# Twelve early down products spread over twelve pairs: one 128-expert tile of each, where both tiles of six pairs were made early, in a layer of pooling, window attention and product-key experts on one Trainium2 core

## The chip, the cores and the metric

The kernel runs on one core of one Trainium2 chip. The metric is the device time of one execution in microseconds (us), and the time of a kernel is the median of its runs. TensorE is the matrix engine, VectorE, ScalarE and GpSimd the other three that compute; SyncE (SP) issues most of the DMAs. In rows of the profile they are PE (PEld for its weight loads), DVE, ACT, POOL and SP.

## What is computed

One layer for 1024 tokens of width 1024, all in float32. First a mixer (a projection, multi-scale pooling, window attention with sinks, sigmoid gates, an output projection), then the product-key experts, then a norm:

```python
x = x + merged @ w_out[l]
x = x + peer_layer(rms_norm(x, g_ffn[l]), ...)
return rms_norm(x, g_final)

# peer_layer: 8 heads pick 16 of 128*128 experts for each token
gates = jax.nn.softmax(vals, axis=-1)
u = jnp.take(expert_down, eb, axis=0)
act = jax.nn.gelu(jnp.einsum('td,thkd->thk', hb, u).astype(jnp.float32))
wv = (gb * act).astype(expert_up.dtype)
vv = jnp.take(expert_up, eb, axis=0)
return jnp.einsum('thk,thkd->td', wv, vv)
```

So each token needs, for its 128 chosen experts, a dot product with a row of `expert_down` and a weighted sum of rows of `expert_up`.

## The kernel before

The eight blocks of 128 tokens are served in two ways. Three blocks (`DB = 3`) go **by rows**: for each of 128 choices GpSimd gathers one row of 4 KB per token (512 KB in all) by an indirect DMA, and VectorE forms the dot product (kind "dot", L1672) or adds the weighted row (kind "up", L1684). That is 3 x 2 x 128 = 768 rows (`NROW`), in the order block 0 dot, block 0 up, block 1 dot and so on. Five blocks (`ND = 5`, 640 tokens, `DT`) go **densely**: all 16384 experts are multiplied, and a table of gates, zero for experts not chosen, weights the result.

The dense work runs over `NPAIR = 64` pairs of tiles; pair p has the tiles (p, 0) and (p, 1), each of 128 experts. For a tile, the down product makes `abank` (experts x 640 tokens) in two halves of 256 and 384 tokens (`SPLIT`), 8 x 3 matmuls each. Three matmuls stand in for one of full precision: each float32 operand is split into a high part (ScalarE's copy to float32r: `tdown_hi`, L1569; `tup_hi`, L1577; `w_hi`, L1595) and a low part (the difference: `tdown_lo`, L1482, and `tup_lo`, L1486, on GpSimd; `w_lo`, L1724, on VectorE). ScalarE takes the gelu of `abank` into `w` (L1588), VectorE multiplies by the gates (`weights`, L1720) and makes the low part (`weights_rest`, L1724). The up product of the pair (`up_product`, L1546 to L1548) goes over five token blocks t, 12 matmuls of 512 columns each, into `ybank`, of which two pairs exist; VectorE adds each to `y` (`add_y`, L1731).

The order on each engine is written out. TensorE, for pair p: the first half of tile (p+1, 0), up product t = 0, second half, t = 1, first half of (p+1, 1), t = 2, second half, t = 3, t = 4. VectorE: the last addition of pair p-1, then five parts of the pair's rows in shares 3, 2, 1, 3, 1, with an addition, the weights of (p+1, 0), an addition and their low part, an addition, the weights of (p+1, 1), an addition and their low part between them. GpSimd: four parts of the gathers in shares 2, 3, 2, 3, followed by `down_rest(p+1, 1)`, `up_rest(p+1, 0)`, `down_rest(p+2, 0)` and `up_rest(p+1, 1)`; the gathers go into a ring of eight rows (`RU = 8`). ScalarE makes the high parts and gelus in the matching order. `rows_of_pair` deals the 768 rows to the pairs by `SHARE`.

**Early down products.** While the mixer's last work runs, TensorE has room. There the mixer makes the down products of twelve tiles (`PRE`, `NPRE`), keeps them in DRAM (`scr["pre"]`), and in the experts' loop those tiles are left out of the loads, the splits and `down_half`; instead SP loads the result into `w` (`load_pre`, L1413), and ScalarE's gelu works on it in place (L1582). The pair ahead of an early pair (where its down product would have been made) gets fewer rows. It is called a light pair here.

Who waits for whom is counted by semaphores that only rise: `down_low` and `down_high` (splits done), `a_ready` (a down product done), `gl_ready` (a gelu done), `w_ready`, `w_low`, `y_ready`, `y_added`. Since early tiles don't count in some of them, `normal(p)` gives how many pairs ahead of p are not early.

Of the kernel before, what the change touches and what calls it, by code (L numbers as in the profile page):

```python
# [11 lines left out]
NG = T // TG  # L12
# [61 lines left out]

PRE = list(range(4, NPAIR, 10))
NPRE = 2 * len(PRE)
LAST = NG * NTILE + NPRE

# [39 lines left out]
def mixer(nc, io, scr):  # L118

    with ExitStack() as ctx:  # L120
# [233 lines left out]
        def _(sp):  # L354
# [4 lines left out]
            def load_tile(n):  # L359
                if n >= RING:  # L360
                    sp.wait_ge(w_low, n - RING + 1)
                g, i = divmod(n, NTILE)
                src = io["tiles"][i] if g < NG else io["downT"][2 * PRE[i // 2] + i % 2]
                sp.dma_start(raw[:, n % RING], src).then_inc(tile_in[n % RING], 16)
# [917 lines left out]

SHARE = [3 if p + 1 in PRE else 10 for p in range(NPAIR)]

# [71 lines left out]

def normal(p):

    return p - sum(n < p for n in PRE)


def experts(nc, io, scr, kept, late):
# [8 lines left out]
    with ExitStack() as ctx:  # L1371
# [32 lines left out]
        def _(sp):  # L1404
            def load_tdown(p, q):
                if p in PRE:
                    return
                sp.wait_ge(down_low, 2 * (normal(p) - 1) + q + 1)
                sp.dma_start(tdown[:, q], io["downT"][2 * p + q]).then_inc(tdown_in[q], 16)

            def load_pre(p, q):
                sp.wait_ge(w_low, 2 * (p - 1) + q + 1)
                sp.dma_start(w[:, q], scr["pre"][2 * PRE.index(p) + q]).then_inc(pre_in[q], 16)  # L1413

# [25 lines left out]
            for p in range(NPAIR):  # L1440
# [7 lines left out]
                if p + 3 < NPAIR:  # L1448
                    load_gates(p + 3)
                if p + 2 in PRE:  # L1450
                    for q in range(2):
                        load_pre(p + 2, q)
# [17 lines left out]
        def _(pool):  # L1470
# [7 lines left out]
            def down_rest(p, q):  # L1478
                if p in PRE:
                    return  # L1480
                pool.wait_ge(down_high, 2 * normal(p) + q + 1)
                nc.gpsimd.tensor_tensor(tdown_lo[:, q], tdown[:, q], tdown_hi[:, q].bitcast(F32), ALU.subtract).then_inc(down_low, 1)  # L1482
# [33 lines left out]
        def _(pe):  # L1516
            def down_half(p, q, half):
                if p in PRE:
                    return
                if half == 0:  # L1520
                    pe.wait_ge(down_low, 2 * normal(p) + q + 1)
                    if q:
                        pe.wait_ge(gl_ready, 2 * p + 1)
                    elif p:
                        pe.wait_ge(gl_ready, 2 * (p - 2 if p - 1 in PRE else p - 1) + 2)
                a, b = SPLIT[half]
# [34 lines left out]
        def _(act):  # L1561
            def down_high_of(p, q):

                if p in PRE:
                    return
                act.wait_ge(tdown_in[q], 16 * (normal(p) + 1))
                if p:
                    act.wait_ge(a_ready, 2 * (normal(p) - 1) + q + 1)
                nc.scalar.activation(tdown_hi[:, q], tdown[:, q], ACT.Copy).then_inc(down_high, 1)  # L1569
# [9 lines left out]
            def expert_gelu(p, q):  # L1579
                if p in PRE:  # L1580
                    act.wait_ge(pre_in[q], 16 * (PRE.index(p) + 1))
                    nc.scalar.activation(w[:, q], w[:, q], ACT.Gelu_apprx_tanh).then_inc(gl_ready, 1)  # L1582
                    return
                act.wait_ge(a_ready, 2 * normal(p) + q + 1)
                if p:
                    act.wait_ge(w_low, 2 * (p - 1) + q + 1)
                for half, (a, b) in enumerate(SPLIT):
                    ins = nc.scalar.activation(w[:, q, a * P:b * P], abank[:, half, 0:(b - a) * P], ACT.Gelu_apprx_tanh)  # L1588
                ins.then_inc(gl_ready, 1)
# [270 lines left out]
```

## Time and profile before

| | us |
|---|---|
| median of 3 runs | 3027.0 |
| lowest, highest | 3024.17, 3028.58 |
| profiled execution | 3019.19 |
| its span (first to last instruction) | 3017.4 |

The profiled execution is one more run. Around its span lie 1.8 us. The mean granted clock of TensorE is 0.972 of full speed. Of the span TensorE is busy 94%, VectorE 77%, ScalarE 31%, GpSimd 70%; the experts' loop runs from about 1243 us to 3003 us. How to read the rows: times are us from the start of the span; an instruction's row has its start, its length, engine, line and operation, what it writes and reads, and in brackets the idle time of its engine before it with what ended it. A mean over the whole span says little here, as the mixer and the loop have different limits; a row of a stretch or of an instruction has to be read with its place in the pair.

### The profile page before, as it was taken

Reading aid. Unit: us, or ns where it says so; the run is one execution under the profiler, and the core shown is the slowest. Engines: PE = TensorE matmul, PEld = TensorE weight load, DVE = VectorE, ACT = ScalarE, POOL = GpSimd, SP = SyncE. Lnnn points to the kernel's source line nnn. Section 1 sums busy time; section 2 is a strip of 40 time slices with the busy share of each in tenths; the row PEclk is TensorE's granted clock in tenths of the full one; section 3 lists DMA queues with packets and bytes.
Section 4 is the critical chain, followed back from the end, with each engine's and each line's share of the span. In section 5 each row is a group of like instructions: output and inputs, shape, how many; then the busy total and the mean of one; then the engine's idle time right before and its main releaser. Section 6 shows DMA issues by size and latency. Waiting matters only on the chain.

```text
span 3017.4 us, 40171 instructions
## 1 busy us (share of the span) xinstructions
PE 2844.6 (94%) x15235; PEld 2477.6 (82%) x15235; DVE 2336.3 (77%) x4348; ACT 937.1 (31%) x1356; POOL 2124.3 (70%) x1552
## 2 busy tenths in 40 slices
PE   7999898999899799899999998999999989999996
PEld 6678777677689688889998997899899979989995
DVE  1332298345499899588999999898899979889998
ACT  4232433232332399322222222222222222222221
POOL 4324576338568799778887886888688868878883
PEclk9899999899899899999999999999999999999998
DMA  3112412112322377989998997999899979989996
GB/s 140 43 63 91 168 64 70 42 50 98 112 87 94 120 238 237 332 310 330 347 349 315 342 336 289 335 342 341 311 343 336 346 266 339 348 311 341 335 337 219
DMA packets 267584, 717.92 MB, mean 238 GB/s; under 512 B 20864, under 2 KB 104064, under 8 KB 267392
## 3 DMA queue, kind: packets, MB, share of 16 engines
q0 software_dynamic: 110912, 403.75, 35.8%
q1 hardware_dynamic: 156480, 311.61, 30.6%
q8 instruction: 121, 1.98, 0.2%
q14 instruction: 71, 0.58, 0.1%
HBM read 657.86 MB, written 57.41 MB: 237 GB/s over the span
## 4 chain that ended last, share of the span: by engine, by line
PE 34%; DVE 8%; POOL 7%; DMA 6%; issue 3%; ACT 1%; DVEq 0%; SPq 0%; ACTq 0%
PE abank L1530 6%; PE abank L1532 6%; PE abank L1531 6%; PE ybank L1546 6%; PE ybank L1547 5%; PE ybank L1548 5%; POOL up L1475 3%; DVE acc L1684 3%; DMA up<-in_down,e_idx 3%; POOL tdown_lo L1482 2%; DMA up<-in_up,e_idx 2%; DVE up L1672 2%; DVE e_y L1731 1%; POOL tup_lo L1486 1%; DMA w<-all_pre 1%
## 5 line engine op out<-in xcount | busy, mean ns | idle before, releaser
L1530 PE MATMUL abank<-m_hT,tdown_hi 128*128 128x384 f32 (+1 forms) x1856 | 576.4, 311 | 15.0 <-ACT w L1588 9.0
L817 POOL TENSOR_TENSOR m_wlo<-m_raw,m_whi 128x1024 fp32r<-128x1024 f32 x128 | 309.5, 2425 | 379.9 <-ACT m_whi L622 376.7
L1532 PE MATMUL abank<-m_hT,tdown_lo 128*128 128x384 f32 (+1 forms) x1856 | 575.9, 310 | 0.0
L1531 PE MATMUL abank<-m_hlo,tdown_hi 128*128 128x384 f32 (+1 forms) x1856 | 574.9, 310 | 0.0
L1546 PE MATMUL ybank<-tup_hi,w_hi 128*128 128x512 f32 x1280 | 509.1, 398 | 45.5 <-DVE e_y L1731 32.7
L1684 DVE SCALAR_TENSOR_TENSOR acc<-up,e_act,acc 128x1024 f32<-128x1024 f32 x381 | 489.7, 1285 | 65.9 <-DMA up<-in_up,e_idx 43.4
L1672 DVE CUSTOM_DVE_ANT_0 up<-up,acc 128x1024 f32<-128x1024 f32 x384 | 457.0, 1215 | 97.8 <-DMA up<-in_down,e_idx 95.2
L1547 PE MATMUL ybank<-tup_lo,w_hi 128*128 128x512 f32 x1280 | 506.2, 396 | 0.0
L1548 PE MATMUL ybank<-tup_hi,w_lo 128*128 128x512 f32 x1280 | 504.2, 394 | 0.0
L1475 POOL DMA_INDIRECT up<-in_up,e_idx x384 | 396.9, 1033 | 106.0 <-issue 92.4
L1475 POOL DMA_INDIRECT up<-in_down,e_idx x384 | 399.1, 1039 | 99.3 <-issue 88.9
L1731 DVE TENSOR_TENSOR e_y<-e_y,ybank 128x512 f32<-128x512 f32 x640 | 408.9, 678 | 5.3 <-PE ybank L1548 4.5
L1530 PEld LDWEIGHTS abank<-m_hT,tdown_hi 128*128 128x128 f32 x1856 | 353.9, 191 | 25.1 <-issue 10.0
L1531 PEld LDWEIGHTS abank<-m_hlo,tdown_hi 128*128 128x128 f32 x1856 | 354.6, 191 | 9.9
L1482 POOL TENSOR_TENSOR tdown_lo<-e_tdown,tdown_hi 128x1024 fp32r<-128x1024 f32 x116 | 281.4, 2426 | 112.6 <-ACT tdown_hi L1569 110.6
L1486 POOL TENSOR_TENSOR tup_lo<-e_tup,tup_hi 128x1024 fp32r<-128x1024 f32 x128 | 308.3, 2409 | 66.7 <-ACT tup_hi L1577 64.7
L1588 ACT ACTIVATE w<-abank 128x256 f32<-128x256 f32 x232 | 88.9, 435 | 856.5 <-PE abank L1532 693.5
L1532 PEld LDWEIGHTS abank<-m_hT,tdown_lo 128*128 128x128 f32 x1856 | 353.6, 191 | 0.0
L436 PE MATMUL bank<-m_hT,m_whi 128*128 128x512 f32 (+2 forms) x848 | 326.7, 385 | 11.6 <-POOL m_wlo L817 7.9
L1546 PEld LDWEIGHTS ybank<-tup_hi,w_hi 128*128 128x128 f32 x1280 | 244.1, 191 | 98.6 <-DVE e_y L1731 38.0
L438 PE MATMUL bank<-m_hT,m_wlo 128*128 128x512 f32 (+2 forms) x848 | 319.7, 377 | 0.0
L437 PE MATMUL bank<-m_hlo,m_whi 128*128 128x512 f32 (+2 forms) x848 | 319.3, 377 | 0.0
(226 smaller groups left out, 4714.6 us busy)
## 6 DMA issues: line engine op xcount, KB each, us to landing
e_tup<-in_up SPq DMA_DIRECT2D x128, 512.0 KB
m_raw<-in_tiles SPq DMA_DIRECT2D x116, 512.0 KB, 3.3
e_tdown<-in_downT SPq DMA_DIRECT2D x116, 512.0 KB
gates<-all_table SPq DMA_DIRECT2D x64, 640.0 KB
all_table<-t_out SPq DMA_DIRECT2D x9, 4096.0 KB, 14.7
m_raw<-in_downT SPq DMA_DIRECT2D x12, 512.0 KB, 3.7
up<-in_down,e_idx POOLq DMA_INDIRECT x384
up<-in_up,e_idx POOLq DMA_INDIRECT x384
```

Of the source, the lines that this page charges most:

```text
L1475: nc.gpsimd.indirect_dma_start(up[:, n % RU], None, io["up" if kind == "up" else "down"], bass.IndirectOffsetOnAxis(idx[:, b, k:k + 1], 0) ...
L1482: nc.gpsimd.tensor_tensor(tdown_lo[:, q], tdown[:, q], tdown_hi[:, q].bitcast(F32), ALU.subtract).then_inc(down_low, 1)
L1486: nc.gpsimd.tensor_tensor(tup_lo[p % 2][:, q], tup[:, q], tup_hi[p % 2][:, q].bitcast(F32), ALU.subtract).then_inc(up_low, 1)
L1530: nc.tensor.matmul(out, tdown_hi[:, q, at], h2T_hi[:, k, a:b], start=k == 0, stop=False)
L1531: nc.tensor.matmul(out, tdown_hi[:, q, at], h2T_lo[:, a:b, at], start=False, stop=False)
L1532: ins = nc.tensor.matmul(out, tdown_lo[:, q, at], h2T_hi[:, k, a:b], start=False, stop=k == KD - 1)
L1546: nc.tensor.matmul(out, w_hi[r][:, q, ts], tup_hi[r][:, q, ds], start=q == 0, stop=False)
L1547: nc.tensor.matmul(out, w_hi[r][:, q, ts], tup_lo[r][:, q, ds], start=False, stop=False)
L1548: ins = nc.tensor.matmul(out, w_lo[r][:, q, ts], tup_hi[r][:, q, ds], start=False, stop=q == 1)
L1672: nc.vector.tensor_tensor_reduce(out=src, in0=src, in1=h2_row[:], scale=1.0, scalar=0.0, op0=ALU.mult, op1=ALU.add, accum_out=act_of[:, b, ...
L1684: nc.vector.scalar_tensor_tensor(out=acc[:], in0=src, scalar=act_of[:, b, k:k + 1], in1=acc[:], op0=ALU.mult, op1=ALU.add).then_inc(row_us ...
L1731: nc.vector.tensor_tensor(part, part, ybank[n % 2 * 2 + i][:], ALU.add).then_inc(y_added, 1)
```

## The change

`PRE` is now a list of tiles: tile 0 of the pairs 4, 9, 14, ... 59. Twelve tiles are made early, as before, but they were both tiles of the pairs 4, 14, ... 54. The pair ahead of each takes 6 shares of rows where it took 3, a full pair 10. That is 592 shares in all where there were 598: 12.97 rows in a full pair (12.84), 7.78 in a light one (3.85). `normal` gives way to four functions that count tiles: how many computed tiles stand ahead of (p, q) in the order of the loop (`nth`), how many of the same q (`nth_in`), the count at which the last computed tile of the same buffer was done (`last_in`), and the last computed tile before this one (`last_before`). All waits on `down_low`, `down_high`, `a_ready`, `tdown_in`, `pre_in` and `gl_ready` are put through them. The orders on the engines are the same.

```diff
-PRE = list(range(4, NPAIR, 10))
-NPRE = 2 * len(PRE)
+PRE = [(p, 0) for p in range(4, NPAIR, 5)]
+NPRE = len(PRE)
...
-                src = io["tiles"][i] if g < NG else io["downT"][2 * PRE[i // 2] + i % 2]
+                src = io["tiles"][i] if g < NG else io["downT"][2 * PRE[i][0] + PRE[i][1]]
...
-SHARE = [3 if p + 1 in PRE else 10 for p in range(NPAIR)]
+SHARE = [6 if (p + 1, 0) in PRE else 10 for p in range(NPAIR)]
...
-def normal(p):
-
-    return p - sum(n < p for n in PRE)
+def nth(p, q):
+
+    return 2 * p + q - sum(tile < (p, q) for tile in PRE)
+
+
+def nth_in(p, q):
+
+    return p - sum(tile[1] == q and tile < (p, q) for tile in PRE)
+
+
+def last_in(p, q):
+
+    return nth(*max((n, q) for n in range(p) if (n, q) not in PRE)) + 1
+
+
+def last_before(p, q):
+
+    return max((n, r) for n in range(p + 1) for r in range(2) if (n, r) < (p, q) and (n, r) not in PRE)
...
             def load_tdown(p, q):
-                if p in PRE:
+                if (p, q) in PRE:
                     return
-                sp.wait_ge(down_low, 2 * (normal(p) - 1) + q + 1)
+                sp.wait_ge(down_low, last_in(p, q))
...
-                sp.dma_start(w[:, q], scr["pre"][2 * PRE.index(p) + q]).then_inc(pre_in[q], 16)
+                sp.dma_start(w[:, q], scr["pre"][PRE.index((p, q))]).then_inc(pre_in[q], 16)
...
-                if p + 2 in PRE:
-                    for q in range(2):
+                for q in range(2):
+                    if (p + 2, q) in PRE:
                         load_pre(p + 2, q)
...
             def down_half(p, q, half):
-                if p in PRE:
+                if (p, q) in PRE:
                     return
                 if half == 0:
-                    pe.wait_ge(down_low, 2 * normal(p) + q + 1)
-                    if q:
-                        pe.wait_ge(gl_ready, 2 * p + 1)
-                    elif p:
-                        pe.wait_ge(gl_ready, 2 * (p - 2 if p - 1 in PRE else p - 1) + 2)
+                    pe.wait_ge(down_low, nth(p, q) + 1)
+                    if 2 * p + q:
+                        n, r = last_before(p, q)
+                        pe.wait_ge(gl_ready, 2 * n + r + 1)
```

The same pattern is applied to `down_rest`, `down_high_of` and `expert_gelu`.

## Rows read from the trace of the kernel before

**Rows 1.** The page, busy tenths in 40 slices of the span, TensorE.

```profile
PE   7999898999899799899999998999999989999996
```

**Rows 2.** Waits of TensorE from 1240 us on: total us, times, longest.

```profile
PE ybank L1546 <- DVE e_y L1731: 32.7, 10, 6.5
PE ybank L1546 <- DVE w_lo L1724: 12.7, 8, 2.8
PE abank L1530 <- ACT w L1588: 7.1, 1, 7.1
```

**Rows 3.** Windows: stretch, us, busy PE, PEld, DVE, ACT, POOL; PEclk, DMA share, GB/s.

```profile
1299.50:1347.70 48.20, 43.69 (x219) 37.74 (x218) 39.93 (x63) 11.54 (x16) 32.38 (x24) 0.96 0.84 304
1571.10:1617.60 46.50, 43.18 (x219) 37.57 (x218) 42.09 (x47) 11.77 (x16) 30.91 (x23) 0.96 0.85 309
1850.30:1897.30 47.00, 42.32 (x218) 36.41 (x217) 41.10 (x62) 11.55 (x16) 31.00 (x24) 1.00 0.89 334
2120.60:2169.80 49.20, 44.08 (x217) 37.73 (x218) 40.05 (x47) 11.54 (x16) 32.81 (x25) 0.97 0.82 295
2392.60:2452.60 60.00, 46.63 (x218) 39.62 (x217) 47.14 (x67) 15.67 (x20) 35.33 (x26) 0.89 0.76 284
2675.50:2723.20 47.70, 43.64 (x218) 37.53 (x217) 42.04 (x63) 11.78 (x16) 32.06 (x25) 0.96 0.85 313
1812.50:1850.30 37.80, 30.70 (x158) 27.86 (x157) 33.48 (x47) 10.59 (x14) 23.84 (x18) 0.86 0.69 240
1645.40:1673.30 27.90, 27.90 (x159) 25.44 (x158) 25.54 (x27) 6.80 (x10) 23.39 (x18) 1.00 0.94 337
```

**Rows 4.** Timeline of TensorE in pair 16, a full one: start us, us.

```profile
1645.42 0.39 PE L1546 MATMUL ybank<-tup_hi,w_hi 128*128 128x512 f32 x1
...
1648.17 0.34 PE L1530 MATMUL abank<-m_hT,tdown_hi 128*128 128x384 f32 x1
...
1652.36 0.39 PE L1546 MATMUL ybank<-tup_hi,w_hi 128*128 128x512 f32 x1
...
1670.39 0.28 PE L1530 MATMUL abank<-m_hT,tdown_hi 128*128 128x256 f32 x1
...
1673.27 0.39 PE L1546 MATMUL ybank<-tup_hi,w_hi 128*128 128x512 f32 x1
```

**Rows 5.** Timelines of GpSimd, VectorE and TensorE in light pair 13 (starts 1596.0).

```profile
1600.34 2.40 POOL L1482 TENSOR_TENSOR tdown_lo<-e_tdown,tdown_hi 128x1024 fp32r<-128x1024 f32 x1 [0.49 <-ACT tdown_hi L1569]
1602.89 1.36 POOL L1475 DMA_INDIRECT up<-in_up,e_idx  x1
...
1608.50 1.29 DVE L1684 SCALAR_TENSOR_TENSOR acc<-up,e_act,acc 128x1024 f32<-128x1024 f32 x1 [3.09 <-DMA up<-in_up,e_idx]
...
1610.44 0.80 PE L1546 MATMUL ybank<-tup_hi,w_hi 128*128 128x512 f32 x1 [3.32 <-DVE e_y L1731]
```

**Rows 6.** Timeline of TensorE where light pair 3 starts.

```profile
1326.73 0.80 PE L1546 MATMUL ybank<-tup_hi,w_hi 128*128 128x512 f32 x1 [2.06 <-DVE w_lo L1724]
1327.32 0.63 PE L1547 MATMUL ybank<-tup_lo,w_hi 128*128 128x512 f32 x1
```

**Rows 7.** Timelines of GpSimd and VectorE late in full pair 16.

```profile
1667.43 2.42 POOL L1482 TENSOR_TENSOR tdown_lo<-e_tdown,tdown_hi 128x1024 fp32r<-128x1024 f32 x1
1670.04 0.82 DVE L1720 TENSOR_TENSOR w<-w,gates 128x640 f32<-128x640 f32 x1
```

**Rows 8.** Timeline of VectorE in pair 54, where rows turn from dot to up.

```profile
2723.96 2.37 DVE L1679 TENSOR_TENSOR e_act<-e_act,e_gate 128x128 f32<-128x128 f32 x1 [0.45 <-ACT e_act L1613]
```

**Rows 9.** Timelines of VectorE and GpSimd late in pair 12, ahead of light pair 13.

```profile
1593.09 0.82 DVE L1720 TENSOR_TENSOR w<-w,gates 128x640 f32<-128x640 f32 x1
1593.82 1.28 DVE L1731 TENSOR_TENSOR e_y<-e_y,ybank 128x512 f32<-128x512 f32 x2
1595.02 0.82 DVE L1724 TENSOR_TENSOR w_lo<-w,w_hi 128x640 fp32r<-128x640 f32 x1
...
1597.44 2.41 POOL L1486 TENSOR_TENSOR tup_lo<-e_tup,tup_hi 128x1024 fp32r<-128x1024 f32 x1 [10.88 <-ACT tup_hi L1577]
```

More of the change, by code:

```diff
@@ L1478, in down_rest @@
             def down_rest(p, q):
-                if p in PRE:
+                if (p, q) in PRE:
                     return
-                pool.wait_ge(down_high, 2 * normal(p) + q + 1)
+                pool.wait_ge(down_high, nth(p, q) + 1)
                 nc.gpsimd.tensor_tensor(tdown_lo[:, q], tdown[:, q], tdown_hi[:, q].bitcast(F32), ALU.subtract).then_inc(down_low, 1)
@@ L1517, in down_half @@
             def down_half(p, q, half):
-                if p in PRE:
+                if (p, q) in PRE:
                     return
                 if half == 0:
-                    pe.wait_ge(down_low, 2 * normal(p) + q + 1)
-                    if q:
-                        pe.wait_ge(gl_ready, 2 * p + 1)
-                    elif p:
-                        pe.wait_ge(gl_ready, 2 * (p - 2 if p - 1 in PRE else p - 1) + 2)
+                    pe.wait_ge(down_low, nth(p, q) + 1)
+                    if 2 * p + q:
+                        n, r = last_before(p, q)
+                        pe.wait_ge(gl_ready, 2 * n + r + 1)
                 a, b = SPLIT[half]
@@ L1562, in down_high_of @@
             def down_high_of(p, q):
-                if p in PRE:
+                if (p, q) in PRE:
                     return
-                act.wait_ge(tdown_in[q], 16 * (normal(p) + 1))
+                act.wait_ge(tdown_in[q], 16 * (nth_in(p, q) + 1))
                 if p:
-                    act.wait_ge(a_ready, 2 * (normal(p) - 1) + q + 1)
+                    act.wait_ge(a_ready, last_in(p, q))
                 nc.scalar.activation(tdown_hi[:, q], tdown[:, q], ACT.Copy).then_inc(down_high, 1)
@@ L1579, in expert_gelu @@
             def expert_gelu(p, q):
-                if p in PRE:
-                    act.wait_ge(pre_in[q], 16 * (PRE.index(p) + 1))
+                if (p, q) in PRE:
+                    act.wait_ge(pre_in[q], 16 * (p - nth_in(p, q) + 1))
                     nc.scalar.activation(w[:, q], w[:, q], ACT.Gelu_apprx_tanh).then_inc(gl_ready, 1)
                     return
-                act.wait_ge(a_ready, 2 * normal(p) + q + 1)
+                act.wait_ge(a_ready, nth(p, q) + 1)
                 if p:
```

## The prediction, made before the changed kernel was run

> **What bounds the kernel now.** I read the slices of the page first. From the sixteenth of forty the work is the experts' loop over 64 pairs, and there TensorE is busy nine tenths and more [rows 1]. The waits of TensorE in that loop come next [rows 2]: 52.5 us in all, and they have three kinds. 32.7 us (ten times) end with a VectorE addition into y (L1731), 12.7 us (eight times) with the low part of the weights (w_lo, L1724), and 7.1 us once with a gelu of ScalarE (L1588). Then the windows from pair to pair [rows 3]. A "pair" below is the stretch from the first up product of pair p (L1546) to that of pair p+1. A full pair takes 27.9 us with TensorE busy for all of it. The six stretches that hold a light pair (3, 13, ... 53, the pairs ahead of an early one) and the pair before it take 48.2, 46.5, 47.0, 49.2, 60.0 and 47.7 us, together 298.6, at clocks of 0.89 to 1.00. The reader should see that nothing is lost in full pairs and that almost all of the loss sits in these six and in pair 21.
>
> **What TensorE needs.** In a full pair [rows 4] the first up product starts at 1645.42, the larger half of the first down product at 1648.17, the second up product at 1652.36; the smaller half of the next down product at 1670.39, and the next pair at 1673.27. So the larger half costs 4.19 us, the smaller 2.88, one down tile 7.07, and the whole pair 27.85. The smaller half of tile 0 lies at the end of the pair before. Two down tiles gone make a two-pair stretch of 2 x 27.85 - 14.14 = 41.56 us; one gone makes 48.63, split as 24.97 (before) and 23.66 (light). Floor of today's six: 6 x 41.56 = 249.4. Their loss is 298.6 - 249.4 = 49.2 us; pair 21 loses 37.8 - 27.85 = 9.95. Sum of losses today: 59.2. The floor of the whole loop doesn't change: twelve tiles are left out either way, so **the change can only move the 59.2**.
>
> **Part 1, the mixer.** Twelve early tiles are loaded, split, multiplied and stored as before; only their addresses differ. Nothing, both ends nothing: same counts and sizes.
>
> **Part 2, inside the light pair.** Today a light pair needs 27.85 - 4.19 - 7.07 = 16.6 us of TensorE, but its y additions come late. The trace of pair 13 shows why [rows 5]: GpSimd has two low parts back to back with almost no gathers, so the gather at 1602.89 lands for VectorE only at 1608.50 (5.6 us later, 3.09 idle), the addition behind it is late, TensorE waits 3.32 us at 1610.44, and its clock then falls. After the change the light pair lasts 23.66 us and has 8 rows in VectorE's parts of 2, 2, 0, 3, 1. With s its start: the y additions of the previous pair to s+1.3, two rows and two additions to 5.1 (1.3 us a row, 1.28 two additions, 0.82 the weights and w_lo each [rows 5, 9]), two rows to 7.7, weights 8.5, additions 9.8, w_lo 10.6, first of three rows 11.9. The next two come from gathers behind one more gather and the tdown_lo that starts 4.3 us into pair 13 [rows 5], 5.0 to 7.4 after the change: at about s+7.5 and 9.1, and land 5.6 us later: 13.1 and 14.7, so the rows end at 16.0 and the additions at 17.3. TensorE needs them for its last up product at 4 x 2.75 + 7.07, about s+18. It is in time by 0.7 us; with landings 1.5 us later (the DMAs carry 8 rows where there were 4) it waits 0.8. I take 0.4 us for each of twelve, bounds 0 and 2: 5 us (0 to 24), where today the ten waits of this kind average 3.3.
>
> **Part 3, the entry.** Before a light pair TensorE lacks the 2.88 us of the small half and is ready for the next up product after 24.97 us, while VectorE and GpSimd still have a full pair's work. Today this is the w_lo wait: eight, 12.7 us, 1.6 each, up to 2.8 [rows 2, 6]; there will be twelve such entries where there are six. A second thing is new. Tile 1 of the early pair is now computed, so GpSimd makes its low part in the entry, behind the gelu that follows the larger half. In a full pair [rows 7] that tdown_lo runs 1667.43 to 1669.85, 22.0 to 24.4 us into the pair, and VectorE's weights start right behind it, at 1670.04. Where the two meet, VectorE's instruction ends only after GpSimd's: a multiply of just 128 x 128 takes 2.37 us [rows 8]. At today's entry of pair 12 GpSimd is idle for 10.88 us [rows 9]; the weights start at 1593.09 (22.0 us into the pair), and with two additions and w_lo VectorE is through at 1595.84, 2.75 us later, just before TensorE gets there at 24.97. With tdown_lo in that place (0.5 earlier than in a full pair, since GpSimd stands waiting: 21.5 to 23.9) VectorE goes on at 23.9 and is through at 26.7: TensorE is 1.7 us late. An entry where VectorE arrives later than 23.9 loses nothing to this, and is late by the old amount, 2.2 at pair 2 (27.2 us to the product at 1326.73 [rows 6] from the start at 1299.5 [rows 3]). I take 1.8 for each of eleven (the twelfth is pair 42's, part 5): 20 us. Bounds 0.8 and 2.8: 9 to 31.
>
> By the Trainium skill, page "SBUF — State Buffer", section "SBUF: two separate sides", VectorE and GpSimd share a port pair under an exclusive lock, and a VectorE op with two SBUF inputs that meets a GpSimd op waits for the whole instruction. By that rule every entry is held as above; without it an entry would cost what it costs today, about 1.2, and the entries together 13 us instead of 20. The 2.37 us multiply [rows 8] agrees with the rule.
>
> **Part 4, clock.** The granted clock falls to 0.5 (1.2 of 2.4 GHz) after some waits: after the entry wait of 2.06 us a product lasts 0.63 us [rows 6] where it lasts 0.39 in a full pair [rows 4], and of the six stretches only the one at 1850.3 averages 1.00 [rows 3]. The light pairs' waits over 3 us do it too [rows 5]. In a stretch of 48.2 us at 0.96, 1.9 us are lost to it; I take 1.8 a drop. With waits of 1.8 I expect one at two or three entries: 4 us (bounds 0 and 21, a drop at each).
>
> **Part 5, ends of blocks.** With 768 rows over 592 shares instead of 598, rows 256 and 512 still end in pairs 21 and 42, at the same places. Pair 21 keeps its 9.95 us (7.1 of it the gelu wait [rows 2]). Pair 42 keeps its y wait of 6.5 us, the longest of that kind [rows 2], and the low clock behind it, 3 us (of the 6.6 us that 0.89 takes from 60.0 [rows 3] about half): together 9.5, its entry included. What pair 43 loses beside it (today's 60.0 against 48 elsewhere) has its cause in the starved gathers of part 2 and mostly goes. Row 640, where VectorE turns from dot products to sums, moves from pair 54 into light pair 53; ScalarE's gelu and the multiply [rows 8] put some 3 us into VectorE's line there: 2 us more for TensorE. The same turn leaves pairs 31 and 32 about 2 us behind, as today (49.2 against 47 [rows 3]).
>
> **Part 6, queues.** SP's load of the precomputed tile now waits for w_lo of tile 0 only, which is long done; the wait for tile 1's, which held the loads queued behind it (tdown and tup of later pairs), goes. The new wait counts follow the same orders of tiles. Full pairs get 13 rows a little more often than 12: VectorE is busy 25.5 of 27.9 us and DMA 0.94 at 337 GB/s [rows 3], so VectorE's idle time covers it (0.13 row of 1.3 us, 0.17 us a full pair, if that is gone). A light pair moves 5 gathers and one tile fewer in 7.1 us less, 6.8 MB or 325 GB/s over 20.8 us, not above a full pair.
>
> **Sum.** 5 (light) + 20 (entries) + 4 (clock) + 9.95 + 9.5 (block ends) + 2 (row 640) + 2 (pairs 31, 32) = 52.5 us of loss where there is 59.2: 7 us gained. Against the profiled execution's own 3019.2 us this is 3012; the median of the runs shown is 3027.0, 7.8 above it, so **3020 us**.
>
> **Rivals.** (a) *All waits fold into the slack*: VectorE reaches the weights ahead of GpSimd, or after it without harm; entries 0.8 us each, light pairs 0, no drops. 9 + 23.5 = 33 of loss, 26 gained: 3001. For it: pair 12 today enters with no wait [rows 9]. Against: the w_lo waits average 1.6 [rows 2]. (b) *The entries take back the gain*: TensorE waits twelve times where it waited six, each near 2.4 us, and the clock falls after each (1.8 more): 11 x 4.2 = 46, and 5 + 23.5: 75, 16 lost: 3043. It decides from 2.8 us an entry, clock included: 11 x 2.8 + 5 + 23.5 is today's 59.2. For it: a wait of 2.06 brought the clock down [rows 6]. Against: w_lo waits average 1.6 [rows 2]. (c) *The gathers stay late in the light pair*: 0.6 us more in each, 12 x 0.6: the gain is gone and the time stays at 3027. (d) *It doesn't do what it says*: had the early tiles not been dropped from TensorE's line the loop would grow by 7.07 us each, to 3112; the conditions on (p, q) in all four engines agree, so I give it nothing.
>
> **How the numbers follow.** The forecast's case gets 0.45, (a) 0.16, (b) 0.20, (c) 0.19. The forecast's own range, 3012 to 3027, comes from entries between 1.1 and 2.4 us. To hold 8 in 10 it reaches to (a) and (b): 3001 to 3043. About 0.2% (6 us) is what a measurement can tell from no change. Faster: (a) and two thirds of the forecast's case (0.30), together 0.46, and 0.01 of (c): 0.47. Same: the rest of the forecast's case (0.15) and 0.15 of (c): 0.30. Slower: (b) and the bad end of (c): 0.23.
>
> **What would show it.** Right: no y wait over 1.5 us in light pairs outside 43 and 53; twelve entries, each with a w_lo wait of 1 to 2 us; GpSimd's tdown_lo just ahead of VectorE's weights in them; two-pair stretches near 51 us; pairs 21 and 42 as before. Wrong: entry waits under 0.5 or over 2.5, a clock below 0.97 in most stretches, waits for gathers over 1 us in the light pairs' three rows, or any wait of TensorE in full pairs.

## The result, and the profile after

| | before | after |
|---|---|---|
| median of the runs | 3025.4 us (6 runs, 3022.7 to 3028.6) | **3041.4 us** (6 runs, 3032.1 to 3045.8) |
| profiled execution: time, span | 3019.2, 3017.4 us | 3043.1, 3041.3 us |
| TensorE waits from 1240 us on: y, w_lo, gelu | 32.7, 12.7, 7.1 us [rows 2] | 33.4, 28.6, 6.9 us |

The ratio is 1.0047 (95% interval 1.0032 to 1.0061): slower by about 14 us (the medians lie 16 apart). The forecast was 3020 and faster. The time lies inside its range, close to the upper end, on the wrong side of no change.

The page of after (engine totals, then TensorE's slices) shows the same work with more time around it:

```profile
PE 2851.4 (94%) x15235; PEld 2477.7 (81%) x15235; DVE 2336.6 (77%) x4348; ACT 937.1 (31%) x1356; POOL 2124.6 (70%) x1552
...
PE   7999899999899799999999998999999989999996
```

The waits of TensorE from 1240 us on (total us, times, longest) answer to [rows 2]:

```profile
PE ybank L1560 <- DVE e_y L1745: 33.4, 18, 7.3
PE ybank L1560 <- DVE w_lo L1738: 28.6, 14, 2.9
PE abank L1544 <- ACT w L1602: 6.9, 1, 6.9
```

The w_lo waits rose from eight to fourteen, 12.7 to 28.6 us. That was forecast in kind. The y waits were to fade and did not: 18 of them, 33.4 us.

Windows of after from pair to pair (columns as in [rows 3]): entry 2 and light 3, entry 12, light 13 and full 14, entry 57 and light 58.

```profile
1296.90:1323.70 26.80, 25.21 (x135) 22.41 (x133) 23.35 (x40) 5.86 (x9) 19.08 (x15) 1.00 0.84 329
1323.70:1348.70 25.00, 24.09 (x133) 21.24 (x134) 21.86 (x33) 6.82 (x9) 20.81 (x16) 1.00 0.95 345
1568.20:1596.10 27.90, 25.16 (x135) 22.36 (x133) 25.24 (x27) 5.85 (x9) 19.95 (x16) 1.00 0.85 329
1596.10:1623.50 27.40, 25.63 (x132) 22.34 (x133) 21.28 (x25) 6.67 (x9) 19.27 (x14) 0.94 0.80 282
1623.50:1651.40 27.90, 27.90 (x159) 25.45 (x158) 24.34 (x26) 6.80 (x10) 23.07 (x18) 1.00 0.96 345
2827.20:2855.40 28.20, 25.29 (x134) 22.31 (x132) 25.24 (x27) 5.86 (x9) 20.05 (x17) 1.00 0.85 332
2855.40:2886.70 31.30, 28.50 (x133) 24.55 (x134) 23.31 (x26) 6.78 (x9) 21.35 (x15) 0.84 0.83 290
```

The forecast's floors serve as a ruler: 24.97 us for an entry, 23.66 for a light pair, 27.85 for a full one. (Where both tiles are early, a light pair's floor is 41.56 - 24.97 = 16.59.) A full pair stands on its floor, 27.9. Entries run 26.8 to 28.2, these lights 25.0 to 31.3. Summed over the loop's first 63 pairs, length less floor, in us:

| kernel (profiled execution) | entries | lights | full | sum |
|---|---|---|---|---|
| before | 18.4 | 30.9 | 11.2 | 60.5 |
| after | 38.5 | 36.5 | 12.0 | 87.0 |
| forecast for after | 20 + 9.5 (pair 42) | 5 + 2 (row 640) | 9.95 + 2 | 48.5, and 4 of clock |

Before is the 59.2 of the forecast, counted over all pairs. The 26.5 us more than before are the whole difference of the two profiled executions (23.9; the loop of after starts 2.6 us earlier). The medians differ by 16 only, since before's profiled execution is 6 us under its median and after's 2 over: some 8 of the 26.5 us are chance. Of the 34.5 us by which the forecast (52.5) missed, 25 to 29 lie in the light pairs and 9 in the entries.

### The profile page after: what moved, and what is told of

Its sections match the earlier page's. It is cut to its first block, busy times and chain, and to the rows that moved or that the text cites. A ratio compares the mean times of both kernels' runs of the same rounds, so it can differ in the third digit from the quotient of the medians.

```text
span 3041.3 us, 40171 instructions
## 1 busy us (share of the span) xinstructions
PE 2851.4 (94%) x15235; PEld 2477.7 (81%) x15235; DVE 2336.6 (77%) x4348; ACT 937.1 (31%) x1356; POOL 2124.6 (70%) x1552
## 4 chain that ended last, share of the span: by engine, by line
PE 15%; DVE 10%; DMA 10%; POOL 8%; issue 5%; ACT 2%; SPq 0%; DVEq 0%; ACTq 0%
POOL up L1490 4%; DMA up<-in_up,e_idx 4%; DMA up<-in_down,e_idx 4%; DVE acc L1698 4%; DVE up L1686 3%; PE abank L1544 3%; PE abank L1546 3%; PE abank L1545 3%; POOL tdown_lo L1497 3%; PE ybank L1560 3%; DMA w<-all_pre 2%; PE ybank L1561 2%; PE ybank L1562 2%; DVE e_y L1745 2%; POOL tup_lo L1501 1%
## 5 line engine op out<-in xcount | busy, mean ns | idle before, releaser
L1560 PE MATMUL ybank<-tup_hi,w_hi 128*128 128x512 f32 x1280 | 512.5, 400 | 62.1 <-DVE e_y L1745 33.4
L436 PE MATMUL bank<-m_hT,m_whi 128*128 128x512 f32 (+2 forms) x848 | 326.7, 385 | 11.9 <-POOL m_wlo L817 8.1
```

The lines of the kernel that those rows point to most:

```text
L1560: nc.tensor.matmul(out, w_hi[r][:, q, ts], tup_hi[r][:, q, ds], start=q == 0, stop=False)
```

## The experiments

All but e10 and e12 start from the kernel after. Ratios are to the kernel before.

**e1: the precomputed tile's load ahead of the gates.** In the light pairs of after one chain is late. Timelines of pairs 12 and 13 of after (13 starts at 1596.1; start us, us, engine and line; in brackets idle time and what ended it): SP's issues, ScalarE, GpSimd, VectorE, TensorE.

```profile
1594.07 0.33 SPq L1437 DMA_DIRECT2D gates<-all_table  x1
1594.44 0.43 SPq L1428 DMA_DIRECT2D w<-all_pre  x1
...
1603.80 0.74 ACT L1596 ACTIVATE w<-w 128x640 f32<-128x640 f32 x1 [8.04 <-DMA w<-all_pre]
1604.44 1.04 ACT L1583 ACTIVATE tdown_hi<-e_tdown 128x1024 fp32r<-128x1024 f32 x1
...
1605.56 2.68 POOL L1497 TENSOR_TENSOR tdown_lo<-e_tdown,tdown_hi 128x1024 fp32r<-128x1024 f32 x1 [5.92 <-ACT tdown_hi L1583]
1608.38 1.36 POOL L1490 DMA_INDIRECT up<-in_up,e_idx  x1
...
1614.45 2.68 DVE L1698 SCALAR_TENSOR_TENSOR acc<-up,e_act,acc 128x1024 f32<-128x1024 f32 x2 [4.33 <-DMA up<-in_up,e_idx]
...
1617.77 0.50 PE L1560 MATMUL ybank<-tup_hi,w_hi 128*128 128x512 f32 x1 [1.77 <-DVE e_y L1745]
```

SP issues the load of the precomputed tile right behind the gates' load, and it lands 9.4 us after its issue, for the gelu at 1603.80 (7.7 us into the pair). ScalarE takes its work in the order written, so the high part of tdown stands behind that gelu, for which ScalarE idles 8.04 us; GpSimd does too, so the low part (5.92 idle) and the gathers behind it wait as well; VectorE idles 4.33 for a row, and the y addition behind the row holds TensorE 1.77. In pair 13 of before the load was issued at 1594.31 and its gelu ran 4.3 us later (timelines of SP and ScalarE of before):

```profile
1594.31 1.88 SPq L1413 DMA_DIRECT2D w<-all_pre  x2
...
1598.58 0.74 ACT L1582 ACTIVATE w<-w 128x640 f32<-128x640 f32 x1 [1.22 <-DMA w<-all_pre]
```

There tdown_lo starts at 1600.34 and the gather is issued at 1602.89 [rows 5], against 1605.56 and 1608.38 here. Over all: in before the first of the two loads reaches its gelu in 4.3 to 4.8 us; in after it takes 4.8 to 6.3 us in the five light pairs ahead of which GpSimd issues two gathers in the entry's last 6 us, and 7.7 to 9.8 in the seven with three. e1 moves the load alone:

```diff
+                for q in range(2):
+                    if (p + 2, q) in PRE:
+                        load_pre(p + 2, q)
                 if p + 3 < NPAIR:
                     load_gates(p + 3)
-                for q in range(2):
-                    if (p + 2, q) in PRE:
-                        load_pre(p + 2, q)
```

> Edit: on the SP queue the load of the precomputed tile is issued ahead of the pair's gate load, so it waits for the low weights of tile 0 (done some 16 us into the entry pair) and no longer for the weights of tile 1 (24 to 26 us into it). In the changed kernel the gelu on that tile comes 3.2 to 5.0 us into a light pair where two gathers were issued in the 6 us ahead of the load, and 6.1 to 8.2 us where three were; light pairs of the first kind last 23.8 to 25.0 us, of the second 25.7 to 31.2. Theory A (the late load holds ScalarE, behind it GpSimd's low part of tile 0 of the next pair, behind that the gathers): the gelu comes under 2.5 us into every light pair, the seven long light pairs fall to some 24.5 us each, 26 us in all and a few more of low clock: 3012 to 3018. Theory B (the row gathers are late because the DMAs are full, and the load is only late beside them): the light pairs stay within 1 us of what they are, 3035 to 3041. The waits at the entries stay in both.

Measured: 3023.5 us, ratio 1.0002 (0.9986 to 1.0019): the whole loss of the change is gone, though the time is above theory A's 3018. The light pairs lose 12.0 us where they lost 36.5; the entries lose 44.9 where they lost 38.5, most of it in pairs 17 (2.6 more) and 42 (1.9); why, no run shows. The same places in e1 (timeline of pairs 12 and 13, which starts at 1596.6), then its waits of TensorE:

```profile
1584.68 1.04 SPq L1428 DMA_DIRECT2D w<-all_pre  x1
1594.57 0.33 SPq L1437 DMA_DIRECT2D gates<-all_table  x1
...
1596.17 0.72 ACT L1596 ACTIVATE w<-w 128x640 f32<-128x640 f32 x1
...
1600.16 2.40 POOL L1497 TENSOR_TENSOR tdown_lo<-e_tdown,tdown_hi 128x1024 fp32r<-128x1024 f32 x1
1602.72 0.95 POOL L1490 DMA_INDIRECT up<-in_up,e_idx  x1 [0.16 <-issue]
```

```profile
PE ybank L1560 <- DVE w_lo L1738: 29.5, 14, 2.9
PE ybank L1560 <- DVE e_y L1745: 20.6, 8, 9.1
```

The load goes out 9.8 us earlier, its gelu waits for nothing, GpSimd has its low part 5.4 us earlier, and the y waits fall from 18 to 8. Of the 12.0 us left in the light pairs 9.8 are the low clock: windows at 0.5 that begin, but for a rest from pair 42, beside the w_lo wait just ahead.

**e6: the load late, but still ahead of the gates.** This keeps e1's order on SP and adds `sp.wait_ge(w_ready, 2 * (p + 2))` ahead of the load, so that it goes out about when it does in after.

> Edit: the load of the precomputed tile is issued at the late time of the changed kernel (after the weights of tile 1) but ahead of the 640 KB of gates, not behind them. In the changed kernel it takes 4.8 to 6.3 us to the gelu in dot stretches and 7.7 to 9.8 us in up stretches; with the early issue it is off the path. Theory G (it waits behind the gates' bytes): 640 KB at some 340 GB/s are 1.9 us, so the gelu comes about 2 us sooner in all of them, up stretches included, 5 to 8 us after the issue, and the seven long light pairs lose 1 to 2 us less each: 3030 to 3036. Theory R (it waits behind the row gathers of which three, not two, were just issued): the time to the gelu moves by under 1 us, 3036 to 3042. If neither, and only the order on the queue counts, it comes at once as with the early issue: 3020 to 3026.

Measured: 3026.3 us, 1.0013 (0.9999 to 1.0026), better than theory G had it. The gelu comes 1.5 to 4.8 us into the light pair (after: 3.2 to 8.2); from the issue it takes 5.0 us in the mean, in after 7.7. The lights lose 16.9 us (the entries 44.7, as in e1). So of the 24.5 us that e1 wins in the light pairs, about 20 come from not standing behind the gates' 640 KB, and 5 from the earlier time.

**e2: tile 1 early in place of tile 0.** Rival for the entries: if TensorE has the small half of tile 0 as filling ahead of a light pair, the entry wait goes.

```diff
-PRE = [(p, 0) for p in range(4, NPAIR, 5)]
+PRE = [(p, 1) for p in range(4, NPAIR, 5)]
-SHARE = [6 if (p + 1, 0) in PRE else 10 for p in range(NPAIR)]
+SHARE = [6 if (p + 1, 1) in PRE else 10 for p in range(NPAIR)]
```

> Edit: the early tile of each of the twelve pairs is tile 1 instead of tile 0. Both halves of its down product lie inside the light pair, so the entry pair keeps its 27.85 us of TensorE and the light pair needs 20.8. Theory C (the w_lo wait at the entry exists because TensorE lacks the small half of tile 0 there while VectorE has a full pair's rows): the w_lo waits of 1.5 to 2.9 us at the twelve entries go, 27 us, and return at most in part as waits inside the light pair. The load of the precomputed tile now waits for the low weights of tile 1, as late as can be; by theory A ScalarE is held for it only late in the pair, where it costs less. Expected: 3015 to 3035. Rival: VectorE's load over the two pairs is what counts, wherever TensorE's gap lies; then the y waits grow by what the w_lo waits lose and the time stays at 3035 to 3045.

Measured: 3075.1 us, 1.0176 (1.0153 to 1.02), a miss for both. Its waits:

```profile
PE ybank L1560 <- DVE e_y L1745: 72.6, 13, 6.2
PE ybank L1560 <- DVE w_lo L1738: 5.2, 3, 2.7
```

The entries do become clean: 27.9 us, a full pair's floor, but for pair 42 (and 28.6 in pair 22). The light pairs take it back and more (timelines of light pair 13, which starts at 1606.4):

```profile
1613.57 0.77 ACT L1602 ACTIVATE w<-abank 128x256 f32<-128x256 f32 x2 [8.19 <-PE abank L1546]
...
1615.36 2.41 POOL L1497 TENSOR_TENSOR tdown_lo<-e_tdown,tdown_hi 128x1024 fp32r<-128x1024 f32 x1 [6.40 <-ACT tdown_hi L1583]
```

Tile 0 is computed now, so ScalarE waits for its down product, 7.1 us into the pair, before it makes the high part of tdown; GpSimd idles 5.7 to 6.9 us for that in each of the twelve, the gathers come late behind it, and TensorE waits 5.0 to 5.9 us for y. From ScalarE's copy on it is the chain of e1 again, with another start: no gelu waits for the early load here.

**e3 and e4: eight shares for the entry and eight for the light pair.** Fewer rows ahead of the entry's weights; e4 has e1's order too.

```diff
-SHARE = [6 if (p + 1, 0) in PRE else 10 for p in range(NPAIR)]
+SHARE = [8 if (p + 1, 0) in PRE or (p + 2, 0) in PRE else 10 for p in range(NPAIR)]
```

> Edit: shares of rows 8 in the entry pair and 8 in the light pair, where they are 10 and 6; the sum is the same. Entries in the stretches where rows are of kind up wait 2.6 to 3.0 us for w_lo, those in dot stretches 1.5 to 1.8. Theory C (VectorE's 13 rows at the entry): 2.6 rows fewer of 1.2 to 1.4 us end VectorE's weights 3 us earlier, the w_lo waits at the entries fall under 0.5; the light pair gets 2.6 rows more, for which its y waits show whether there was room. If the late load rules the light pair (theory A), the extra rows there add at most 1 us each: 3015 to 3035. Rival (light pairs are bound by VectorE): they grow by 3 us each and the time goes to 3050.

> Edit: the early issue of the precomputed tile's load and the shares 8 and 8 together. If A and C both hold, the entries' waits (27 us) and the long light pairs (26 us) both go, less some 12 us for the rows that moved into the light pairs: 2995 to 3010. If the light pairs are bound by VectorE or by the DMAs: 3030 and more.

Measured: e3 3034.5 us, 1.0033 (1.0019 to 1.0047); e4 3032.4, 1.0035 (1.0019 to 1.0051). Entries fall from 38.5 to 13.1 us of loss, and lights rise from 36.5 to 50.7, with y waits of 1.0 to 4.6 us. In e4 entries fall from e1's 44.9 to 15.2, and lights rise from 12.0 to 44.4. So rows moved into the light pair save more in the entry than they cost there while the late load holds the light pairs anyway (e3), and cost more than they save once it does not (e4). e3 also shows the meeting of GpSimd and VectorE that the forecast had expected (timelines of entry 12 of e3, which starts at 1571.9):

```profile
1593.34 2.40 POOL L1497 TENSOR_TENSOR tdown_lo<-e_tdown,tdown_hi 128x1024 fp32r<-128x1024 f32 x1 [7.24 <-ACT tdown_hi L1583]
1593.43 2.98 DVE L1734 TENSOR_TENSOR w<-w,gates 128x640 f32<-128x640 f32 x1
...
1597.54 0.87 DVE L1738 TENSOR_TENSOR w_lo<-w,w_hi 128x640 fp32r<-128x640 f32 x1
```

The weights take 2.98 us where they take 0.82 [rows 9]. Of the entries the seven whose weights start by 21.2 us take 25.0 to 25.1; four whose weights start at 21.6 to 23.5, beside that low part, all take 26.6 to 26.7.

**e5: fewer rows in the entry only, spread over the full pairs.** With e1's order:

```diff
-SHARE = [6 if (p + 1, 0) in PRE else 10 for p in range(NPAIR)]
+SHARE = [60 if (p + 1, 0) in PRE else 92 if (p + 2, 0) in PRE else 100 for p in range(NPAIR)]
```

> Edit: the early issue of the precomputed tile's load, and shares of rows 92 in the entry pair, 60 in the light one, 100 in a full one (12, 8 and 13 to 14 rows). With the early issue alone the entries lose 44.9 us against what TensorE needs (w_lo waits of 1.6 to 2.9), the light pairs 12.0, the full ones 10.6. One row fewer at the entry is 1.2 to 1.4 us of VectorE. If VectorE's rows set the entry waits, the entries lose 13 us less, light pairs the same; the full pairs get 13.2 rows instead of 13.0 and keep their cover: 3008 to 3016. Rival: full pairs have no room (VectorE's rows with the waits for gathers fill 27.8 us): the full pairs lose 10 us more: 3022 to 3028.

Measured: 3021.2 us, 0.9998 (0.9983 to 1.0013), between the two expectations. Entries lose 31.7 us, 13 less than in e1, as expected; full pairs 17.3 in place of 10.6. Six of the entry waits are 1.49 or 1.50 us, with weights that start anywhere from 22.4 to 23.4 us in: the held weights of e3 again.

**e9: GpSimd's low part behind the weights.** On top of e5 GpSimd makes the low part of tile 1 in an entry only after w_lo.

```diff
-                if p + 1 < NPAIR:
+                if p + 1 < NPAIR and (p + 1, 0) not in PRE:
                     down_rest(p + 1, 1)
...
+                if (p + 1, 0) in PRE:
+                    pool.wait_ge(w_low, 2 * p + 2)
+                    down_rest(p + 1, 1)
```

> Edit: as the kernel with the early load and shares 92, 60 and 100, and in a light pair GpSimd makes the low part of the next pair's tile 1 after the part of gathers that followed it, and only once VectorE's low weights of the pair are done. In that kernel eight entries wait 1.5 us each to a few hundredths, with VectorE's weights started at 22.3 to 23.4 us and the low weights done at 26.6, 3.2 to 4.3 us later where 2.8 is usual: the trace shows the weights running until GpSimd's low part of the tile ends. Theory L (this meeting holds them): the low weights end 2.8 us after the start of the weights, the entries with an early start wait 0 to 0.9, 6 us gained over all, 3012 to 3017. Rival: GpSimd, now later by 3 to 4 us, delays the next tile's product or the gathers and the light pairs lose what the entries win: 3020 to 3028.

Measured: 3018.8 us, 0.998 (0.9966 to 0.9995). Timelines of entry 12 of e9, which starts at 1568.1:

```profile
1579.16 3.58 DVE L1737 TENSOR_TENSOR w<-w,gates 128x640 f32<-128x640 f32 x1
1579.64 2.41 POOL L1501 TENSOR_TENSOR tup_lo<-e_tup,tup_hi 128x1024 fp32r<-128x1024 f32 x1
...
1593.54 0.82 DVE L1737 TENSOR_TENSOR w<-w,gates 128x640 f32<-128x640 f32 x1
1595.47 0.82 DVE L1741 TENSOR_TENSOR w_lo<-w,w_hi 128x640 fp32r<-128x640 f32 x1
1596.37 2.41 POOL L1497 TENSOR_TENSOR tdown_lo<-e_tdown,tdown_hi 128x1024 fp32r<-128x1024 f32 x1 [8.09 <-DVE w_lo L1741]
```

The weights of tile 1 are never held now: 0.82 us, and w_lo ends 2.8 us after they start in every entry. Three entries fall to 25.1 to 25.5 us. But in others VectorE starts these weights later than in e5, by up to 2.2 us (entry 12: 25.5 in place of 23.2 us in), and in the profile the entries' sum stays at 31.9. The rows show why: in six entries (2, 12, 17, 22, 37 and 42) the weights of tile 0, some 11 us in, take 2.5 to 3.6 us, beside GpSimd's tup_lo; in e5 that is so in three (22, 42 and 47). So moving one of GpSimd's steps took one hold away and let another in at the pair's first weights. The time is slightly below before's, but the lead over e5 is not clear of the scatter of the runs, and the profile doesn't show it: its sum of losses (62.1) is above e5's (58.5).

**e7 and e8: other pairs.** Tiles of pairs 6, 11, ... in place of 4, 9, ..., with e1's order (e7), and with e5's shares as well (e8): this takes the block end of pair 42 away from an entry.

```diff
-PRE = [(p, 0) for p in range(4, NPAIR, 5)]
+PRE = [(p, 0) for p in range(6, NPAIR, 5)]
```

> Edit: the early issue, and the early pairs are 6, 11, ... 61 instead of 4, 9, ... 59, so that pair 42, in which the second block of rows ends, is a full pair and no entry. With the early issue alone pairs 42 and 43 take 61.2 us where TensorE needs 48.6: 12.6 lost, 9.1 of it one y wait. If the block's end costs more because it meets an entry, pairs 42 and 43 lose some 10 as two full pairs while the entry beside them costs its usual 3: between 0 and 4 us gained, and turning points of rows move (row 128 into light pair 10): 3018 to 3024. If not: the same time as the early issue alone, 3023 to 3026.

> Edit: early issue, shares 92 and 60 to 100, and early pairs 6, 11, ... 61. If the gains of the two add to that of the early issue: 3003 to 3012. If the full pairs have no room for their rows: 3020 to 3028.

Measured: e7 3034.3 us, 1.0039 (1.0017 to 1.006); e8 3029.2, 1.0021 (1.001 to 1.0032): both are slower than any of the expectations. Pair 42, now full, takes 36.3 us, 8.5 over its floor, where as an entry it takes 35.2, 10.2 over (in e1 37.1, 12.1 over). But the turn at row 128 now lies in light pair 10, which takes 32.6 us (e8: 34.7) with a y wait of 5.3. One end of a block is taken out of the short pairs and another is put in. That explains a part only: e7's profiled execution (3026.6 us) is 8 us under its median, so most of its 11 us over e1 stands in no profile.

**e11: three shares for the light pair in place of six.**

```diff
-SHARE = [6 if (p + 1, 0) in PRE else 10 for p in range(NPAIR)]
+SHARE = [3 if (p + 1, 0) in PRE else 10 for p in range(NPAIR)]
```

> Edit: the changed kernel with shares of 3, not 6, for its twelve light pairs: 4 rows there, 13.8 in a full pair. Full pairs have 13 rows at most today with VectorE 95% busy in 27.85 us; 0.8 row more is 1.1 us of VectorE against 0 to 1 of room. If they are at their limit, 52 pairs lose 0.5 to 1 us each: 3065 to 3095. If there is room, the light pairs' waits go and the time falls to 3010 to 3025.

Measured: 3075.1 us, 1.017 (1.0143 to 1.0196), as the first expectation had it. Its lights lose little, 11.9 us, but full pairs lose 41.6 and entries 68.0. Its waits:

```profile
PE ybank L1560 <- DVE e_y L1745: 42.4, 24, 10.2
PE ybank L1560 <- DVE w_lo L1738: 26.2, 18, 2.8
```

The full pairs have no room for the 36 shares' worth of rows that move into them.

**e10: the old tiles with the new share.** This and e12 start from the kernel before, both tiles of six pairs.

```diff
-SHARE = [3 if p + 1 in PRE else 10 for p in range(NPAIR)]
+SHARE = [6 if p + 1 in PRE else 10 for p in range(NPAIR)]
```

> Edit: the kernel before with shares of 6 for its six light pairs (8 rows where they have 4; full pairs 12.5 instead of 12.8). Its light pairs need 16.6 us of TensorE and last 20.3 to 25.5. If VectorE's work sets them, 3.6 rows of 1.2 to 1.4 us add 4 to 5 us each, some 28 us, and the full pairs give nothing back: 3045 to 3055. If the rows only fill the 3 us in which VectorE waits for a gather there: 3030 to 3038.

Measured: 3040.4 us, 1.0062 (1.0042 to 1.0081), between the two expectations. Each light pair takes 24.3 us or more where before's took 20.3 to 21.6 (pair 43 apart), with y waits of 3.9 to 7.8.

**e12: the old tiles with the early load.** From before, the load of tile 0 goes ahead of the gates, that of tile 1 stays behind:

```diff
+                if p + 2 in PRE:
+                    load_pre(p + 2, 0)
                 if p + 3 < NPAIR:
                     load_gates(p + 3)
                 if p + 2 in PRE:
-                    for q in range(2):
-                        load_pre(p + 2, q)
+                    load_pre(p + 2, 1)
```

> Edit: the kernel before with the load of the first of its two precomputed tiles issued ahead of the gates. There that load takes 4.3 to 4.8 us to its gelu (5.8 to 9.8 in the changed kernel), 2.5 to 3.2 us into the light pair, and few gathers are in flight. If what the changed kernel lost is its own (the queue behind the gates with gathers in flight), this gives little: 3020 to 3027. If the kernel before suffered from it too, ScalarE's copy for GpSimd comes 2 us sooner and the gathers behind it, and each of six light pairs loses 1 to 2 us less: 3012 to 3018.

Measured: **3010.7 us, 0.9961 (0.9947 to 0.9976)**, the fastest of all, below both kernels. Windows of its light pairs 3, 13 and 43 (columns as in [rows 3]), its waits of TensorE, and the loads of pair 13 on SP and at ScalarE:

```profile
1324.70:1343.10 18.40, 16.91 (x84) 14.14 (x85) 17.42 (x25) 6.27 (x8) 16.68 (x11) 1.00 0.90 303
1591.60:1612.50 20.90, 18.21 (x85) 15.08 (x84) 17.71 (x21) 7.71 (x9) 17.44 (x12) 0.92 0.82 279
2419.50:2442.10 22.60, 18.32 (x84) 15.25 (x85) 16.58 (x27) 7.04 (x9) 19.18 (x13) 0.92 0.90 335
```

```profile
PE ybank L1547 <- DVE e_y L1732: 24.7, 9, 7.0
PE ybank L1547 <- DVE w_lo L1725: 13.2, 8, 2.8
```

```profile
1580.93 0.33 SPq L1413 DMA_DIRECT2D w<-all_pre  x1
1589.42 0.33 SPq L1422 DMA_DIRECT2D gates<-all_table  x1
1591.35 0.32 SPq L1413 DMA_DIRECT2D w<-all_pre  x1
...
1592.85 0.72 ACT L1583 ACTIVATE w<-w 128x640 f32<-128x640 f32 x1
...
1599.15 0.72 ACT L1583 ACTIVATE w<-w 128x640 f32<-128x640 f32 x1
```

The first gelu comes 1.2 us into pair 13 (1591.6), where before it came 2.6 us in, and the second is no later than before. The six lights take 117.8 us together, before's 130.4: 12.6 less, of 13.3 in the profiled execution.

## Why the prediction was wrong

**What bounds the kernel, and the floors: right.** TensorE's instructions are the same in number. Full pairs stay at 27.9, and every change of time is a change in the losses around the light pairs. Pair 21 takes 37.4 us (37.8 before) and pair 42 loses 10.2, both as part 5 said (9.95 and 9.5). The 2 us for pairs 31 and 32 did not come (28.3 us, and 27.9 like entry 12); that the full pairs' 12.0 match the forecast's is luck, as pair 10 (29.0) and pair 20 (28.5) fill the place. Row 640 was overpriced: light pair 53 takes 24.3 us, 0.6 over its floor, where I added 2.

**Part 6, the queues: this is the step that failed.** It said that SP's load of the precomputed tile waits for w_lo of tile 0 only, which is long done, and so put its landing at nothing. But SP issues in order, and the gates' load ahead of it waits for the weights of tile 1: these end at 1594.05, SP issues the gates' load at 1594.07 and the tile's at 1594.44. So the load still goes out late, and it stands behind the gates' 640 KB, at a time when the traffic around it is no longer the same. I had read part 2's chain from pair 13 of before, where no gather was issued in the 6 us ahead of the load; its row at GpSimd (tdown_lo 4.3 us into the pair [rows 5]) was the trace of a load whose gelu comes 4.3 us after the issue. After the change two or three gathers are issued in the last 6 us of the entry, and the gelu comes 4.8 to 9.8 us after the load's issue. e1 shows by the result that this is what was lost (36.5 to 12.0), e6 splits it (about 20 for standing behind the gates, 5 for the time). The part's 325 GB/s for a light pair is also wrong: it spreads the bytes over 20.8 us where the pair's floor is 23.66.

**Part 2, the light pair: mis-sized by that.** Taken at 5 us for twelve, with bounds to 24, plus 2 for row 640. In after the lights lose 36.5: 18.6 in y waits, 15.2 in the low clock, 2.7 elsewhere. The gather that I put at s+7.5 is issued in pair 13 at s+12.3 (1608.38). In e1, where the load is in time, it is issued at s+6.1, and one y wait of 0.9 us is left in twelve light pairs. So the working from the gather on holds once its start does. Rival (c) named this mechanism, at 0.6 us a pair more; the lights came out 29 us over the forecast, 2.5 each.

**Part 3, the entries: right in kind, too small, for a reason not quite mine.** Twelve entries with a w_lo wait each, but for pair 42, whose wait is for y: as forecast. I took 1.8 us for each of eleven, 20; they lose 38.5 - 10.2 (pair 42) = 28.3, 2.6 each, inside the bounds. Part 3 took the w_lo waits of before for entry waits; five of the eight are, 8.1 us, which leaves the mean at 1.6. And the lock, VectorE held by GpSimd's low part, hardly acts on the weights. In after they start 23.4 to 24.1 us in at the entries 2, 7, 27, 47 and 52, where VectorE's rows are dot products, and at 25.0 or later at the others, where, but for pair 22 and the end of pair 42, they are sums; GpSimd's low part ends at 23.9 (in pair 42 later, like all else). Only in pair 52 are they held, 1.17 us in place of 0.82. In entry 12 the low part runs 1589.70 to 1592.11:

```profile
1589.70 2.41 POOL L1497 TENSOR_TENSOR tdown_lo<-e_tdown,tdown_hi 128x1024 fp32r<-128x1024 f32 x1 [4.71 <-ACT tdown_hi L1583]
...
1593.23 0.82 DVE L1734 TENSOR_TENSOR w<-w,gates 128x640 f32<-128x640 f32 x1
1595.16 0.86 DVE L1738 TENSOR_TENSOR w_lo<-w,w_hi 128x640 fp32r<-128x640 f32 x1
1596.07 0.50 PE L1560 MATMUL ybank<-tup_hi,w_hi 128*128 128x512 f32 x1 [2.74 <-DVE w_lo L1738]
```

The entry wait comes from VectorE's lateness. My sample, pair 12 of before, with weights at 22.0 us [rows 9], was the earliest of the six entries: in the others they start 23.4 to 31.7 us in. After the change pair 12 has them at 25.0, past the point where TensorE stands. The rows account for these 3.0 us: it has 13 rows where it had 12 (1.4 with the step to the next), VectorE waits 1.66 us for a gathered row, which it did not before, and the first w_lo takes 1.40 us in place of 0.82, beside GpSimd's tup_lo; 0.6 us are won elsewhere.

```profile
1572.91 1.29 DVE L1698 SCALAR_TENSOR_TENSOR acc<-up,e_act,acc 128x1024 f32<-128x1024 f32 x1 [1.66 <-DMA up<-in_up,e_idx]
...
1582.76 1.40 DVE L1738 TENSOR_TENSOR w_lo<-w,w_hi 128x640 fp32r<-128x640 f32 x1
```

e3 and e5 confirm it from the other side: fewer rows shorten the entries, by 25 us (against after) and 13 (against e1). e3 and e5 confirm also that the lock exists, and that it acts on weights that start 21.6 to 23.5 us in. By the Trainium skill, page "SBUF — State Buffer", section "SBUF: two separate sides", the held VectorE instruction waits out the whole of GpSimd's; the 2.98 us of e3, which end 0.7 us after GpSimd's 2.40 do, agree. So do the 3.58 us of e9, though by the trace that instruction starts 0.5 us ahead of GpSimd's. That VectorE comes 1.1 us later with sums (entries 12, 32, 37 and 57) than with dot products fits its rows: a sum starts 1.39 us after the one before it, a dot product 1.14 (both in after). Over an entry's 13 rows this is some 2 us, of which longer waits for gathers in the dot entries (2.7 to 3.4 us against 1.7 to 2.4) give back about half.

**Part 4, clock: 4 us forecast.** Four drops of 3.41 us at half speed follow entry waits (in or at pairs 13, 23, 33 and 58, after 2.74, 2.52, 2.64 and 2.91 us), 6.8 us in all: near. The other drops in the lights begin beside y waits (in pairs 38, 43 and 58), cost 8.5 us and come with part 2's failure. Entry waits of 1.5 to 1.8 brought none.

**Rival (b)**, 3043 us, has the time nearly right: twelve entry waits of about 2.4. But in its sum the light pairs cost 5 us, and every entry a drop of the clock; the runs show 36.5 and four drops. A right total is no proof of a mechanism: by (b) e1 could not have given the loss back.

**The chances.** Slower stood at 0.23, and all but 0.03 of it rested on the entries. What was missing is a price for the landing of the load, bounded from above by a load landed beside gathers. The same loads of before give no such bound: they land 3.5 to 5.3 us after their issue, all with no gather issued in the 6 us ahead.

## What to carry to other kernels

When a step moves, read the queue that its load stands in: what is ahead of it, what traffic runs then, and which in-order engine waits for it. A landing time is only good for a place with the same traffic. And before one pair's timeline serves as the sample for twelve, look at the others of its kind and count its work: pair 12 was the earliest entry of six, and one row more and one wait for a gather turned it from an entry with no wait into one with 2.7.

## What the runs showed that I had not expected

- A load of one precomputed tile behind the gates' load takes 4.3 to 4.8 us from issue to gelu with no gather issued in the last 6 us of the pair, 4.8 to 6.3 with two, 7.7 to 9.8 with three. Among these twelve it goes by the gathers and not by the kind of the rows: the load of light pair 23, with three gathers, takes 9.05 us though dot products stand ahead of it, as they do ahead of the five with two. Ahead of the gates and issued at about the same time the load is up to 5 us faster (e6).
- Removing the cause of a 1.5 us wait in six entries (e9) did not shorten the entries' sum in the profile: the same kind of hold came up at the pair's first weights, up to 3.58 us in place of 0.82.
- The clock fell after entry waits of 2.04 (e1, pair 2) and 2.06 us (before [rows 6]), and did not after 2.79 and 2.84 (after, pairs 17 and 37): the length of the wait alone does not tell.
- Not tried: e12's order with other shares or with e9's step. What e12 still loses in its lights is 18.3 us.
